# Narrow bias tiles stored from eight buffers of their own, and stores awaited in the next stages instead of at the end of the block

## What is computed

```python
bias = jnp.moveaxis(bias_table[bucket], -1, 2)           # used by the dilated attention of layer 1
...
mod = (cond @ ada_w[i] + ada_b[i]).reshape(B, N_MOD, D)
h = rms_norm(x, norm_mix[i]) * (1 + scale1) + shift1
y = mla_mixer(h, ...)                                    # layer 0
proj = h @ w_in                                          # the first thing mla_mixer does, 1024 -> 672
```

## Time and profile before

| | us |
|---|---|
| median of 3 runs | 3579.03 |
| lowest and highest of them | 3574.47 and 3585.44 |
| the profiled execution, own time | 3578.78 |
| its span in the profile | 3577.0 |

### The profile page before, as it was taken

One profiled execution on the slowest core, in us unless ns is written; L12 is line 12 of the kernel. 1 busy time (PEld: TensorE's weight loads), 2 busy tenths in 40 slices (PEclk: granted clock), 3 DMA queues, 4 the chain that ended last, 5 costly groups with the idle time before them and its releaser, 6 DMA issues. The chain is left out here.

```text
span 3577.0 us, 62308 instructions
## 1 busy us (share of the span) xinstructions
PE 3326.7 (93%) x25272; PEld 2575.6 (72%) x25272; DVE 1940.5 (54%) x2404; ACT 1246.7 (35%) x2149; POOL 1273.9 (36%) x721
## 2 busy tenths in 40 slices
PE   6899999999999999799999997888999999999998
PEld 4455678887767677578887886666678887578876
DVE  8457565564454434665664664444366454854344
ACT  3345331224554655221224423322232224142222
POOL 0134334445646453134443230000335443034443
PEclk9899999999999999799999997877999999999999
DMA  6334144443434343244442220000145443123322
GB/s 239 109 89 124 54 153 168 162 169 111 133 109 128 116 120 98 71 158 159 172 159 83 57 60 17 4 4 10 55 147 188 141 153 95 43 77 99 94 94 82
DMA packets 282552, 384.83 MB, mean 108 GB/s; under 512 B 60214, under 2 KB 205274, under 8 KB 271066
## 3 DMA queue, kind: packets, MB, share of 16 engines
q1 hardware_dynamic: 277976, 367.70, 32.1%
q10 hardware_dynamic: 4354, 13.98, 1.0%
HBM read 361.68 MB, written 19.92 MB: 107 GB/s over the span
## 5 line engine op out<-in xcount | busy, mean ns | idle before, releaser
L510 POOL TENSOR_TENSOR w_lo<-w_raw,w_hi 128x1024 fp32r<-128x1024 f32 x294 | 726.7, 2473 | 1113.4 <-ACT w_hi L501 1113.4
L522 PE MATMUL ps<-h_hi,w_hi 128*128 128x512 f32 x2368 | 933.2, 394 | 41.0 <-ACT h_hi L705 13.1
L523 PE MATMUL ps<-h_hi,w_lo 128*128 128x512 f32 x2368 | 929.4, 392 | 0.0
L526 PE MATMUL ps<-h_lo,w_hi 128*128 128x512 f32 x2368 | 852.7, 392 | 0.0
L501 ACT ACTIVATE w_hi<-w_raw 128x1024 fp32r<-128x1024 f32 x294 | 311.8, 1061 | 1124.7 <-PE ps L526 1090.3
L522 PEld LDWEIGHTS ps<-h_hi,w_hi 128*128 128x128 f32 x2368 | 449.6, 190 | 149.5 <-issue 29.4
L526 PEld LDWEIGHTS ps<-h_lo,w_hi 128*128 128x128 f32 x2368 | 449.6, 190 | 94.9
L523 PEld LDWEIGHTS ps<-h_hi,w_lo 128*128 128x128 f32 x2368 | 449.5, 190 | 93.2
L859 DVE TENSOR_TENSOR h_lo<-big,h_hi 128x512 fp32r<-128x512 f32 x100 | 242.7, 2427 | 229.1 <-ACT h_hi L501 229.0
L1785 POOL TENSOR_TENSOR w_lo<-w_raw,w_hi 128x512 fp32r<-128x512 f32 x192 | 249.3, 1310 | 268.9 <-ACT w_hi L1986 265.7
L663 DVE SCALAR_TENSOR_TENSOR big<-yT,cond,big 128x2048 f32<-128x2048 f32 x63 | 173.9, 2760 | 89.9 <-DMA yT<-in_ada_w 89.5
(11 more groups left out here) (480 smaller groups left out, 5599.6 us busy)
## 6 DMA issues: line engine op xcount, KB each, us to landing
w_raw<-in_mlp_w SPq DMA_DIRECT2D x128, 512.0 KB, 3.6
yT<-in_ada_w SPq DMA_DIRECT2D x56, 1024.0 KB, 5.9
w_raw<-in_dil_w_in SPq DMA_DIRECT2D x192, 256.0 KB, 3.0
w_raw<-in_ffn_w_up SPq DMA_DIRECT2D x176, 256.0 KB, 3.1
h_free<-in_ada_w SPq DMA_DIRECT2D x24, 1024.0 KB, 5.0
w_raw<-in_ffn_w_down SPq DMA_DIRECT2D x44, 512.0 KB, 3.6
w_raw<-in_ab_w_in SPq DMA_DIRECT2D x70, 256.0 KB, 2.9
yT<-in_ada_w SPq DMA_DIRECT2D x32, 512.0 KB, 6.2
```

What stands on the lines that cost most here:

```text
L510: self.nc.gpsimd.tensor_tensor(self.w_lo[:, s, :], self.w_raw[:, s, :], self.w_hi[:, s, :].bitcast(F32), ALU.subtract).then_inc(sg["w_spli ...
L522: self.nc.tensor.matmul(out, w_hi, h_hi, start=start, stop=False)
L523: self.nc.tensor.matmul(out, w_lo, h_hi, start=False, stop=False)
L526: return self.nc.tensor.matmul(out, self.w_hi[:, s, lo:lo + P], self.h_lo[:, h, :], start=False, stop=stop)
```

## The change

Three things are done. First, each narrow tile gets a buffer of its own, 256 columns in parts of the work area that hold nothing by then, and the wait for the store of tile x - 2 stands only before wide tiles. Second, ACT's wait for all stores at the end of `start` goes. Third, the same wait (twelve stores on each of two semaphores) is put before the first later instruction that could touch a buffer or the stored bias: on ACT before the first square of `mla`, on DVE before the rotary table is written, on SP before the first `load_bias` of `dilated`. The two semaphores are then given back at the end of `dilated` instead of the end of `start`.

```diff
+        narrow_out = [self.work(n, (256,)) for n in (22016, 22272, 64, 320, 576, 1024, 1280, 1536)]
...
                 def out(x):
                     g, p = tiles[x]
                     w = width(g)
-                    if x >= 2:
+                    stage = narrow_out[p] if g == 2 else bias_out[x % 2]
+                    if x >= 2 and g < 2:
                         act.wait_ge(sg[f"bias_stored{x % 2}"], sg.at(f"bias_stored{x % 2}", 16 * (x // 2)))
...
-                for u in range(2):
-                    act.wait_ge(sg[f"bias_stored{u}"], sg.at(f"bias_stored{u}", 16 * (len(tiles) // 2)))
...
             nc.scalar.preload_act_table_set(LN_EXP)
+            for u in range(2):
+                act.wait_ge(sg[f"bias_stored{u}"], sg.at(f"bias_stored{u}", 16 * 12))
             for m in range(5):
                 act.wait_ge(sg["lat_full"], sg.at("lat_full", m + 1))
...
+            for u in range(2):
+                v.wait_ge(sg[f"bias_stored{u}"], sg.at(f"bias_stored{u}", 16 * 12))
             v.wait_ge(sg["sin_cos"], sg.at("sin_cos", 1))
...
             for n in range(8):
                 load(n)
+            for u in range(2):
+                sp.wait_ge(sg[f"bias_stored{u}"], sg.at(f"bias_stored{u}", 16 * 12))
             sp.wait_ge(sg["ada_sum"], sg.at("ada_sum", 0))
             load_bias(0)
```

## The result

| | before | changed |
|---|---|---|
| median of 10 runs | 3581.86 us | 3575.08 us |
| lowest and highest | 3574.47 and 3587.85 us | 3569.09 and 3579.22 us |
| span of the first profiled execution | 3577.0 us | 3567.6 us |

The ratio is 0.998 with a 95% interval of 0.9971 to 0.999, so the change gained 6.8 us in the medians, and between 3.6 and 10.4 us by the interval. The changed kernel was timed in two more sessions, beside before each time: 0.9974 (0.9961 to 0.9988) and 0.9982 (0.9969 to 0.9994).

The account below looks back on a forecast made before the run. PE bounds the kernel overall, but ACT's store waits end the first block; 1.8 us from buffers plus 1.4 from the landing, zero for added waits, take 3579.03 to a 3575.8 us median, range 3570 to 3583.

Parts of the forecast that it names:

- What bounds the place: End of `start`: ACT ends last by some 4 us, PE being busy 0.45 of 7 us from 112 to 119.
- Part 2, the landing: End of `start`: ACT no longer stands from its last issue, 114.83, to the store's landing, 116.2; worth 1.4 us.
- the rival of the waiting drain: End of `start`: the drain waits for the last stores after all, leaving 1.8 us gained, 3577.0 us; chance 0.04.
- Part 3, the added waits: One pair of waits each on ACT, DVE and SP in later stages: zero cost, bounds 0 and 0.1 us.
- Part 1, the own buffers: Narrow tiles in `start`: eight ACT store waits go, PE then paces ACT, last copy at 112.3 not 114.09; worth 1.8 us.
- the last tile is in PSUM at 112.12: End of `start`: PE's last narrow tile keeps its old time, so ACT's last copy runs 112.3 to 112.7.
- ACT is no longer last: End of `start`: upper bound of the gain, 4.0 us, from 116.77 less PE's drain at 112.2 and 0.57.
- The clock in the projection: Projection in `mla`: the clock's rise scatters around zero gain; begin to end stays 43.8 us, give or take 2.
- eaten: Projection in `mla`: the clock rises no earlier, so half the gain is lost, 1.6 us left, 3577.2 us; chance 0.10.
- helped: Projection in `mla`: the shorter pause before it lets the clock rise at once, gain 5.5 us, 3573.3 us; chance 0.08.
- Does the shift carry: From `mla` to the program's end: weights land in time and semaphores order the rest, so nothing gives the 3.2 us back.
- the slower rival: Recurrent scan, 2171 to 2545 us: the shift puts more work at half clock; 10 us more gives 3580.6; chance 0.14.

Follow-up runs that it names:

- third changed trace: The changed kernel run once more without further edits, its third traced execution; 0.9982 (0.9969 to 0.9994) against the kernel before.
- own_buffers: The kernel before with only a buffer for each narrow tile, the wait for all stores kept at the block's end; 0.9994 (0.9983 to 1.0005) against the kernel before.

## Why the forecast was right, and where it was mis-sized

- **What bounds the place: right.** The hole between 101 us and the projection was ACT's to open: with the store waits gone its last issue came at 108.44 instead of 114.50, and the block ended 7.5 us earlier.
- **Part 2, the landing: right in kind and size.** 1.4 us forecast, 1.45 measured, with the buffers as they were and with buffers of their own. The drain does not wait for DMAs in flight, so the rival of the waiting drain is out.
- **Part 3, the added waits: right.** In the first changed trace nobody waits for the bias stores in `mla` or `dilated`: DVE comes to its pair at 122.21 and ACT at 149.82, 12 us and more behind the landing at 110.1; the wait of POOL for a bias load was 0.9 us before and is 1.0 now. The pause of PE before the projection is 3.45 us, for 3.4 forecast; from the end of ACT's last issue, 108.77, to `gain` it is 0.48, for 0.5.
- **Part 1, the own buffers: right in kind, mis-sized.** The step that failed is "the last tile is in PSUM at 112.12". It took the 6.82 us of sums from one execution as a property of the kernel. While the stores paced ACT, nothing in the trace could have shown that this duration varies, but the text had the cause in hand: it noted that the clock had fallen before the sums, and then followed the clock only into the projection, where it could give or take 2 us, and not into the sums, which by its own account stood on the new path. At the full clock the sums would have been about half as long, 3.4 us less, and the gain 6.6 us instead of 3.2, above the upper bound of 4.0. That bound, "ACT is no longer last", held PE's drain fixed at 112.2 and failed with it. The first changed trace had the last tile in PSUM at 107.71, 4.4 us earlier than forecast: 3.2 from the sums, 0.7 because they began earlier, 0.5 from the five tiles behind them (4.13 us for 4.61). It was the trace read, and not the change, that made the sums 6.82 us: the kernel before had 3.63 too.
- **The first wide stretch** also varies: ACT's first narrow copy came at 98.77 (forecast 101.1), since its last wide tiles, which wait for stores, were copied 2.3 to 2.4 us earlier in that execution, and at 100.92 and 100.49 in the two other traces. It moves nothing, because PE is in its sums then.
- **The clock in the projection: as forecast.** 42.8, 44.4 and 44.4 us against 43.8, 43.9 and 44.1 before, within the 2 us allowed, so neither "eaten" nor "helped" came true there. The clock helped in another place than the one that the rival named.
- **Does the shift carry, and the slower rival.** From `gain` to the end of the span it took 3453.7 to 3460.8 us before and 3458.1 to 3474.2 us after. The medians, below before in all three sessions, say that the shift carries; these traces alone don't show it. The third changed trace, with its `gain` 3.9 us earlier than before's first, had a span of 3587.1, 10 us more. The kernel before has executions of 3590 us as well, so this is put down to scatter; that the change adds nothing to the later stages is not shown.

The page "TensorE: Matmul & The Clock Gate" of the Trainium skill, section "What's actually happening", says of the clock's rise that its point depends on where the first matmul lands and that the same kernel shows different counts of slow matmuls from run to run. The six traces show the same kind of scatter at a fall of the clock: the same 32 matmuls, begun within 2 us of each other, took 3.63 to 6.82 us.

## What to carry to other kernels

When a wait is removed, the work that it was hiding becomes the path, and its duration in one trace may be the duration at one clock level: price each such piece at both levels before setting the bounds. A wait for a store to land at the end of a block costs what is left of the landing (here 1.45 us) and can go to the first reader or writer, if the buffers allow it. And before calling a piece of work hidden, read by how much: here the sums were covered up to 108.5 to 110 us, and doubling them went past it.

## What the runs showed of the hardware

- An engine's drain and the barrier at the end of a block did not wait for a store in flight: ACT's drain took 156 ns at 108.8 us, while the store issued at 108.44 landed at 110.1. In `own_buffers`, where ACT waits for the landing, `gain` came 2.25 us after the last issue; in the changed kernel it came 0.81 us after it.
- With two matmuls on constants in a pause of 1.9 us before it, a dense stretch of 96 recorded matmuls took 41.4 to 42.5 us, for 42.8 to 44.4 without them. At the low clock the two took 3.4 to 3.8 us and held the stretch up, so from `gain` to the stretch's end it took 43.3 to 46.1 us, for 44.7 to 46.3: too little to tell apart.
- 32 one-column matmuls with their weight loads took 3.6 us at the high clock and 6.8 at the low one: they go with the clock although they move one column each. One weight load took 192 ns at the median in the changed kernel's sums (clock 1.00) and 333 ns in those of before (0.50).
